# Latent attention: three roots, one weight split and the last two heads' third transpose chunk moved

## The chip, the cores and the metric

The kernel runs on one core of a Trainium2 chip. The metric is the time of one execution of the whole program on the device, in microseconds (us). The matrix engine (TensorE) is PE, its weight loads are PEld, VectorE is DVE, ScalarE is ACT, GpSimd is POOL, and SP is SyncE, whose queue issues the weight loads.

## The reference, cut to what matters

Two blocks of a network run on one sequence of 512 rows of width 1024 in fp32. The first has a gated MLP beside dilated attention, then a feed-forward part. The second has latent attention, a feed-forward part, an mLSTM mixer and a last feed-forward part. The change touches the latent attention alone:

```
cq  = rms_norm(h @ w_dq);            q = (cq @ w_uq)   -> 16 heads of 96
ckv = rms_norm((h @ w_dkv)[:256]);   kv = (ckv @ w_ukv) -> 16 heads: 64 of k, 64 of v
k = [k, shared rotary 32];  q = rms_norm(q)*gain;  k = rms_norm(k)*gain;  rotate the last 32
p = softmax(q k^T * 96**-0.5, key chunk (of 64) <= query chunk)
y = (p v, heads side by side) @ w_o
```

## The kernel before, in words

The program is written by hand for each engine, with semaphores between them; nothing plans the order but the code. Every large product is three fp32r matmuls (high by high, high by low, low by high), so each unit of weights is split once it has landed: `split_hi` (line 399, work at L408, on ACT) writes the rounded part, `split_lo` (line 410, work at L414, on DVE) the rest. A unit is loaded into a slot once the unit before the last in that slot has been split low; SP waits for this in `load_unit` (line 393).

`mla` (lines 2116 to 2552) is the latent attention. The 16 heads (MH) come in four groups of four. Each group g needs four q products and four kv products ("q", g, t and "kv", g, t, one for each tile t of 128 rows), a square of all q and all k (`squares`, L2326 on ACT, POOL's L2404 for k of groups 2 and 3), row sums (`sums`, L2415 on DVE), means (L2419), the square roots (`roots`, L2330 on ACT, Sqrt), their reciprocals and the scaling of k (`norm`, L2423 to L2429 on DVE) and the rotation (`rotate`, L2435 to L2438). Groups 0 and 1 are made ahead of the first head; groups 2 and 3 in among the heads. Before the change `roots(g)` for g = 1, 2, 3 is called at the end of the iterations n = 0, 4 and 8 of ACT's loop over the heads.

One head n takes these steps:
- PE, `scores(n)` (L2240): query tiles in the order 3, 2, 0, 1 against the keys up to the tile's end, so 512, 384, 128 and 256 columns. Tile 3 goes to PSUM bank 0, tiles 2 and 0 to bank 1, tile 1 to bank 2.
- DVE, `mask` (L2447) adds the mask, takes the row maximum and puts the scores in SBUF (SB); `shift` (L2454) makes the bias of the exponential. `masks(n)` is the masks of tiles 2, 0 and 1 and one shift.
- ACT, `exps(n)` (L2337): four exponentials, in place.
- PE, `turn(n, c)` (L2250): the probabilities are transposed in three chunks, of 4, 4 and 2 blocks. Chunks 0 and 2 go to PSUM bank 3, chunk 1 to bank 4. Chunks 0 and 2 are copied to SBUF by ACT (L2384, counted by `pte`, two for each head), chunk 1 by DVE (L2515, counted by `a1`). As chunk 2 goes into the bank of chunk 0, `turn(n, 2)` waits for the copy of chunk 0.
- PE, `values(n)` (L2262): probabilities by values, to bank 6, with a column of ones for the denominators. Tile 3 needs the copy of chunk 0, tile 2 that of chunk 1, tile 1 that of chunk 2.
- DVE, `normed(n)` (L2464, L2466): divides by the denominators.
- Every second head, PE transposes a pair of heads (job "out", L2223), ACT empties it to `norm_T_hi` (L2312) and DVE makes `norm_T_lo` (L2472).

PE's loop runs one head ahead with the scores:

```
scores(n + 1); turn(n, 0); tr q of head n + 2; turn(n, 1); tr k of head n + 2
turn(n, 2); out; values(n); products of a later group
```

"tr" are transposes of q and k (L2218), emptied by ACT (L2316). The jobs ("q", "kv", "tr", "out") take their banks in turn: the first twenty from 5, 7, 4, 6, the others from 5 and 7 (`bank`, L2182). ACT's loop is, for head n: a split at n = 2, 3, 5, 10 and 13 (`SPLITS`, L2184), copy of chunk 0, tr q, copy of chunk 2, tr k, out, `exps(n + 1)`, products, roots or squares. DVE's is: mask of tile 3 of n + 1 and its shift, copy of chunk 1, the other masks of n + 1, out, sums and split, `normed(n)`, the rest of a group's work.

The first heads: after the kv products of group 1 ACT empties the transposes of heads 0 and 1 (`heads01`, L2367), squares k of group 1 (L2369) and then does `exps(0)`. ACT's `split_hi(u0 + 4)` stands between the first and the second kv product of group 1 (L2365), DVE's `split_lo(u0 + 4)` ahead of the masks of head 0 (L2503). The unit u0 + 4 holds the q weights of group 2, first used at n = 1.

The last heads: for n = 15 the turns, the values and the last "out" are handed on (`tail`, L2293) and run between pieces of the product with w_o, whose first piece needs the masks of all heads to be done (`freed`, L2546).

Of the kernel before, what the change touches and what calls it, by code (L numbers as in the profile page):

```python
# [15 lines left out]
P = 128  # L16
# [26 lines left out]
ACT = mybir.ActivationFunctionType  # L43
# [179 lines left out]
def build(nc, A, out, stop_after=99):  # L223
    with ExitStack() as ctx:
# [1891 lines left out]
        def mla(block, CKV, banks):  # L2116
# [63 lines left out]
            def bank(m):  # L2180

                return (5, 7, 4, 6)[m % 4] if m < 20 else (5, 7)[m % 2]  # L2182

            SPLITS = {2: 5, 3: 6, 5: 7, 10: 8, 13: 9}  # L2184

            @block.sync
# [4 lines left out]
            @block.tensor  # L2191
            def _(pe, ev=ev.copy(), tl=tl.copy(), pex=pex.copy(), a1=a1.copy(), pte=pte.copy(), ond=ond.copy(), fs=fs.copy(), ropes=ropes.copy()):
                def job(what):
                    m = idx[what]
                    same = [i for i in range(m) if bank(i) == bank(m)]
                    if same:
                        last = same[-1]
                        pe.wait_ge(ev.sem, ev.at(emptied[last]))
                        if order[last][0] == "out":
                            pe.wait_ge(tl.sem, tl.at(order[last][1] + 1))  # L2200
                    kind = what[0]
                    if kind == "q":
                        ua = u0 + 2 * what[1]
                        if what == ("q", 0, 0):
                            pe.wait_ge(tl.sem, cq_made)
                        pe.wait_ge(w_lo, ua + 1)
                        group_N(pe, ua, 0, 384, 384, 3, PS[:, bank(m), 0:384], what[2], AH, AL)
                    elif kind == "kv":
                        ub = u0 + 2 * what[1] + 1
                        if what == ("kv", 0, 0):  # L2210
                            pe.wait_ge(tl.sem, ckv_made)
                        pe.wait_ge(w_lo, ub + 1)
                        group_N(pe, ub, 0, 512, 512, 2, PS[:, bank(m), :], what[2], AH, AL, k0=3)
                    elif kind == "tr":
                        j, h = what[1:]
                        pe.wait_ge((ropes, fs)[j].sem, (ropes.at(4 * (h // 4) + 2), fs.at(h // 4 + 1))[j])
                        for t in range(NT):
                            mm = pe.transpose(PS[0:MQK, bank(m), t * P:t * P + P], QK[:, h // 4 % 2, j, t, h % 4, :], IDENT[:, :])  # L2218
                        mm.then_inc(tp.sem, 1)
                    else:  # L2220
                        pe.wait_ge(ond.sem, ond.at(2 * what[1] + 2))
                        for t in range(NT):
                            mm = pe.transpose(PS[:, bank(m), t * P:t * P + P], ON[:, t, :], IDENT[:, :])  # L2223
                        mm.then_inc(tp.sem, 1)

                def compressed():
                    pe.wait_ge(xn.sem, ckv_ready)
                    for k in range(2):
                        for t in range(NT):
                            mm = pe.transpose(PS[:, banks[k], t * P:t * P + P], CKV[:, t, k * P:k * P + P], IDENT[:, :])  # L2230
                        mm.then_inc(tp.sem, 1)

                def scores(n):
                    pe.wait_ge(ev.sem, ev.at(emptied[idx[("tr", 1, n)]]))
                    for i, t in enumerate(ORDER):
                        b, c = S_AT[t]
                        w = (t + 1) * P
                        if n and c == 0:
                            pe.wait_ge(smk.sem, smk.at(4 * n - 4 + (1, 3, 4)[b]))
                        pe.matmul(PS[:, b, c:c + w], QT[:, n % 2, t * P:t * P + P], KT[:, n % 2, 0:w],  # L2240
                                  start=True, stop=True).then_inc(sc.sem, 1)

                def turn(n, c):
                    pe.wait_ge(pex.sem, pex.at(4 * n + RAISED[c]))
                    if c == 2:
                        pe.wait_ge(pte.sem, pte.at(2 * n + 1))
                    elif n:
                        pe.wait_ge((pte, a1)[c].sem, (pte.at(2 * n), a1.at(n))[c])
                    for i, (t, j) in enumerate(CHUNKS[c]):
                        mm = pe.transpose(PS[:, 4 if c == 1 else 3, i * P:i * P + P], SB[:, off[t] + j * P:off[t] + j * P + P], IDENT[:, :])  # L2250
                    mm.then_inc(ptr.sem, 1)

                def values(n):
                    if n:
                        pe.wait_ge(ond.sem, ond.at(n))
                    for t in ORDER:
                        if t == 2:
                            pe.wait_ge(a1.sem, a1.at(n + 1))
                        elif t != 0:
                            pe.wait_ge(pte.sem, pte.at(2 * n + (1 if t == 3 else 2)))  # L2260
                        for j in range(t + 1):
                            mm = pe.matmul(PS[:, 6, t * MV1:t * MV1 + MV1], PT[:, off[t] + j * P:off[t] + j * P + P],  # L2262
                                           VN[:, n // 4 % 2, j, n % 4, :], start=j == 0, stop=j == t)
                    mm.then_inc(pvd.sem, 1)

                for m, what in enumerate(fills[0] + fills[1] + heads01):
                    if m == 2:
                        compressed()
                    job(what)
                scores(0)  # L2270
                for n in range(MH):
                    behind, between, before, gemms = jobs_at(n)
                    if n + 1 == MH:
                        break
                    scores(n + 1)
                    turn(n, 0)
                    for what in behind:
                        job(what)
                    turn(n, 1)
                    for what in between:  # L2280
                        job(what)
                    turn(n, 2)
                    for what in before:
                        job(what)
                    values(n)
                    for what in gemms:
                        job(what)

                def last_turn():
                    for c in range(3):  # L2290
                        turn(MH - 1, c)

                tail.extend((last_turn, lambda: values(MH - 1), lambda: job(("out", MH // 2 - 1))))  # L2293

            @block.scalar
            def _(act):
# [64 lines left out]
                squares(1, 0)  # L2361
                for t in range(NT):
                    empty(("kv", 1, t))
                    if t == 0:
                        split_hi(act, u0 + 4)  # L2365
                act.wait_ge(gcol, 16 * 5)
                for what in heads01:  # L2367
                    empty(what)
                squares(1, 1)  # L2369
                exps(0)  # L2370
                for n in range(MH):
# [4 lines left out]
                    for c in (0, 2):  # L2376
                        if c:
                            for what in behind:
                                empty(what)
                        act.wait_ge(ptr.sem, ptr.at(3 * n + c + 1))  # L2380
                        if n:
                            act.wait_ge(pvd.sem, pvd.at(n))
                        w = len(CHUNKS[c]) * P
                        act.activation(PT[:, 4 * c * P:4 * c * P + w], PS[:, 3, 0:w], ACT.Copy).then_inc(pte.sem, 1)  # L2384
                    for what in between + before:
                        empty(what)
                    if n + 1 < MH:
                        exps(n + 1)
                    for what in gemms:
                        empty(what)  # L2390
                    if n % 4 == 0 and g < 4:
                        roots(g)
                    if n % 4 == 2 and g + 1 < 4:
                        squares(g + 1, 0)
                empty(("out", MH // 2 - 1))
# [11 lines left out]
            def _(dve):  # L2407
# [92 lines left out]
                norm(0)  # L2500
                sums(1, 0)
                rotate(1, 0)
                split_lo(dve, u0 + 4)  # L2503
                mask(0, 3)
                shift(0, slice(3, 4))
                masks(0)
                for n in range(MH):
                    g = n // 4 + 1
                    if n + 1 < MH:
                        mask(n + 1, 3)  # L2510
                        shift(n + 1, slice(3, 4))
                    dve.wait_ge(ptr.sem, ptr.at(3 * n + 2))
                    if n:
                        dve.wait_ge(pvd.sem, pvd.at(n))
                    dve.tensor_copy(PT[:, 4 * P:8 * P], PS[:, 4, :]).then_inc(a1.sem, 1)  # L2515
                    if n + 1 < MH:
                        masks(n + 1)
                    if n % 2 == 0 and n:
# [532 lines left out]
```

## Time and profile before

| what | us |
|---|---|
| median of three runs (lowest, highest) | 1930.77 (1930.56, 1930.82) |
| the profiled execution's own time | 1930.67 |
| its span in the trace | 1928.9 |
| PE busy | 1912.6 |
| DVE busy | 1216.5 |
| ACT busy | 944.2 |
| granted TensorE clock over the span | 1.0 |

The span is the time from the first to the last instruction of the profiled execution; the 1.8 us between it and the execution's own time lie around it. A start time in the rows below is in us from the span's start. PE's matmuls are pipelined and their ends are modelled, so a matmul that was waited for shows as a later start. The heads run from about 866 us (scores of head 0) to 1012 us (last pair), and the products of the groups before them from about 841 us.

### The profile page before, as it was taken

The page shows a single profiled execution, that of the slowest core. Times are in us where ns is not written, and L with a number is a line of the kernel's source. Part 1 is how long each engine was busy: PE and PEld are TensorE (multiplying, and loading weights), DVE is VectorE, ACT ScalarE, POOL GpSimd, SP SyncE. Part 2 cuts the span into 40 slices and gives each one's busy share as a digit, 9 for nine tenths or more (in the row PEclk, how much of TensorE's full clock was granted, in tenths as well). Part 3 has the DMA queues.
Part 4 walks back from the last instruction along what each step waited for, and adds up shares of the span by engine and source line. Part 5 has one row for each costly group of instructions (what it writes and reads, how often), then busy time and mean ns, then how long its engine had stood idle before and what let it go on. Part 6 is the DMA issues. An engine that isn't in the chain of part 4 may idle for free.

```text
span 1928.9 us, 23399 instructions
## 1 busy us (share of the span) xinstructions
PE 1912.6 (99%) x9546; PEld 1624.9 (84%) x9546; DVE 1216.5 (63%) x1653; ACT 944.2 (49%) x1335; POOL 50.3 (3%) x85
## 2 busy tenths in 40 slices
PE   8999999999999999999999999999999999999999
PEld 6889998888888888898888888888888889888887
DVE  5645553345767676976745868667634357776867
ACT  5333334234645445568744644435564546453543
POOL 1000000000000000010000000000000000000000
PEclk9999999999999999999999999999999999999999
DMA  7233322322341431311014142241232223414141
GB/s 249 76 98 97 92 68 97 110 99 88 110 139 38 151 114 62 103 59 46 23 44 131 44 153 93 83 153 44 89 110 68 86 66 109 140 58 153 35 140 68
DMA packets 163397, 182.47 MB, mean 95 GB/s; under 512 B 7681, under 2 KB 125014, under 8 KB 163162
## 3 DMA queue, kind: packets, MB, share of 16 engines
q1 hardware_dynamic: 160746, 176.67, 28.4%
q0 software_dynamic: 2528, 4.29, 0.8%
q8 instruction: 76, 1.25, 0.3%
q14 instruction: 31, 0.25, 0.0%
q10 hardware_dynamic: 16, 0.00, 0.0%
HBM read 175.62 MB, written 2.11 MB: 92 GB/s over the span
## 4 chain that ended last, share of the span: by engine, by line
PE 96%; DVE 2%; ACT 1%; issue 0%; DMA 0%; ACTq 0%; DVEq 0%
PE psum L96 29%; PE psum L98 29%; PE psum L97 29%; PE psum L2262 2%; PE psum L2240 2%; PE psum L2693 1%; PE psum L2250 1%; PE psum L566 1%; DVE weights_lo L414 1%; PE psum L2218 1%; PE psum L2681 0%; PE psum L1013 0%; PE psum L984 0%; PE psum L1005 0%; PE psum L994 0%; PE psum L982 0%
## 5 line engine op out<-in xcount | busy, mean ns | idle before, releaser
L96 PE MATMUL psum<-norm_T_hi,weights_hi 128*128 128x512 f32 (+1 forms) x1440 | 538.3, 374 | 0.2 <-DVE weights_lo L414 0.2
L98 PE MATMUL psum<-norm_T_hi,weights_lo 128*128 128x512 f32 (+1 forms) x1440 | 533.6, 371 | 0.0
L97 PE MATMUL psum<-norm_T_lo,weights_hi 128*128 128x512 f32 (+1 forms) x1440 | 533.3, 370 | 0.0
L414 DVE TENSOR_TENSOR weights_lo<-raw_weights,weights_hi 128x2048 fp32r<-128x2048 f32 (+3 forms) x136 | 299.2, 2200 | 234.0 <-ACT weights_hi L408 233.9
L408 ACT ACTIVATE weights_hi<-raw_weights 128x2048 fp32r<-128x2048 f32 (+3 forms) x136 | 249.4, 1834 | 189.4 <-PE psum L98 189.4
L98 PEld LDWEIGHTS psum<-norm_T_hi,weights_lo 128*128 128x128 f32 x1440 | 271.2, 188 | 46.6
L96 PEld LDWEIGHTS psum<-norm_T_hi,weights_hi 128*128 128x128 f32 x1440 | 271.4, 188 | 45.7 <-DVE weights_lo L414 0.5
L97 PEld LDWEIGHTS psum<-norm_T_lo,weights_hi 128*128 128x128 f32 x1440 | 271.4, 188 | 45.5
L96 PE MATMUL psum<-weights_hi,act_T_hi 128*128 128x512 f32 (+1 forms) x528 | 203.9, 386 | 0.0
L98 PE MATMUL psum<-weights_hi,act_T_lo 128*128 128x512 f32 (+1 forms) x528 | 202.9, 384 | 0.0
L97 PE MATMUL psum<-weights_lo,act_T_hi 128*128 128x512 f32 (+1 forms) x528 | 202.9, 384 | 0.0
L414 DVE TENSOR_TENSOR weights_lo<-scratch,weights_hi 128x2048 fp32r<-128x2048 f32 x66 | 151.2, 2291 | 51.4 <-ACT weights_hi L408 51.4
L408 ACT ACTIVATE weights_hi<-scratch 128x2048 fp32r<-128x2048 f32 x66 | 126.1, 1910 | 100.6 <-PE psum L98 100.6
L1698 ACT ACTIVATE scratch<-psum 128x512 f32<-128x512 f32 x96 | 57.2, 596 | 217.8 <-PE psum L98 217.8
L96 PE MATMUL psum<-weights_hi,norm_T_hi 128*128 128x512 f32 (+3 forms) x352 | 127.9, 363 | 0.9 <-DVE norm_T_lo L608 0.5
L97 PE MATMUL psum<-weights_lo,norm_T_hi 128*128 128x512 f32 (+3 forms) x352 | 125.6, 357 | 0.0
L98 PE MATMUL psum<-weights_hi,norm_T_lo 128*128 128x512 f32 (+3 forms) x352 | 125.6, 357 | 0.0
L96 PEld LDWEIGHTS psum<-weights_hi,act_T_hi 128*128 128x128 f32 x528 | 99.2, 188 | 18.8 <-issue 0.3
L98 PEld LDWEIGHTS psum<-weights_hi,act_T_lo 128*128 128x128 f32 x528 | 99.1, 188 | 18.7
L97 PEld LDWEIGHTS psum<-weights_lo,act_T_hi 128*128 128x128 f32 x528 | 99.2, 188 | 18.6
L96 PE MATMUL psum<-weights_hi,feed_operands 128*128 128x512 f32 x288 | 112.2, 390 | 0.0
L97 PE MATMUL psum<-weights_lo,feed_operands 128*128 128x512 f32 x288 | 112.1, 389 | 0.0
(315 smaller groups left out, 2463.9 us busy)
## 6 DMA issues: line engine op xcount, KB each, us to landing
raw_weights<-in_ffn_w_dram SPq DMA_DIRECT2D x32, 1024.0 KB, 5.4
scratch<-in_ffn_w_dram SPq DMA_DIRECT2D x32, 1024.0 KB, 5.4
raw_weights<-in_w_in_dram SPq DMA_DIRECT2D x26, 512.0 KB, 5.1
raw_weights<-in_w_in_dram SPq DMA_DIRECT2D x11, 1024.0 KB, 5.2
raw_weights<-in_w_up_dram SPq DMA_DIRECT2D x8, 1024.0 KB, 6.7
scratch<-in_w_up_dram SPq DMA_DIRECT2D x8, 1024.0 KB, 6.7
raw_weights<-in_w_down_dram SPq DMA_DIRECT2D x8, 1024.0 KB, 5.4
scratch<-in_w_down_dram SPq DMA_DIRECT2D x8, 1024.0 KB, 5.2
```

What stands on the lines that cost most here:

```text
L96: pe.matmul(out, ah, bh, start=start, stop=False, skip_group_check=more)
L97: pe.matmul(out, ah, bl, start=False, stop=False, skip_group_check=more)
L98: return pe.matmul(out, al, bh, start=False, stop=stop, skip_group_check=more)
L408: act.activation(WH[:, u % 2, 0:c], raw(units[u].slot)[:, 0:c], ACT.Copy).then_inc(w_hi, 1)
L414: dve.tensor_tensor(WL[:, u % 2, 0:c], raw(units[u].slot)[:, 0:c], WH[:, u % 2, 0:c].bitcast(F32), SUB).then_inc(w_lo, 1)
L566: mm = pe.transpose(PS[:, bank, q * P:q * P + P], (X if behind else XN)[:, t, k * P:k * P + P], IDENT[:, :])
L1698: act.activation(h, PS[:, up_banks[f % 4], :], ACT.Relu).then_inc(fr.sem, 1)
L2218: mm = pe.transpose(PS[0:MQK, bank(m), t * P:t * P + P], QK[:, h // 4 % 2, j, t, h % 4, :], IDENT[:, :])
L2240: pe.matmul(PS[:, b, c:c + w], QT[:, n % 2, t * P:t * P + P], KT[:, n % 2, 0:w], start=True, stop=True).then_inc(sc.sem, 1)
L2250: mm = pe.transpose(PS[:, 4 if c == 1 else 3, i * P:i * P + P], SB[:, off[t] + j * P:off[t] + j * P + P], IDENT[:, :])
L2262: mm = pe.matmul(PS[:, 6, t * MV1:t * MV1 + MV1], PT[:, off[t] + j * P:off[t] + j * P + P], VN[:, n // 4 % 2, j, n % 4, :], start=j == 0, ...
L2693: mm = pe.matmul(PS[:, 4 + t, 0:LV + 1], place(h, j)[1][:, (t - j) * P:(t - j) * P + P], VN[:, h % 2, j, :], start=j == 0, stop=j == t)
```

## The change

There are three moves; nothing is computed that was not computed before, and each engine has the same instructions.

1. ACT calls `roots(g)` at n = 1, 5 and 9, between the emptied k transposes and `exps(n + 1)`, where it called them at n = 0, 4 and 8 behind everything else.
2. ACT's `split_hi(u0 + 4)` goes from behind the first kv product of group 1 to behind `heads01`, ahead of `squares(1, 1)` and `exps(0)`. DVE's `split_lo(u0 + 4)` goes from before to behind the masks of head 0.
3. For heads 14 and 15 the third chunk is transposed into the bank that the last "out" job takes (bank 7), where it was bank 3. `turn(14, 2)` waits for the job before in that bank (tr k of head 15) instead of for the copy of chunk 0; `turn(15, 0)` and `turn(15, 2)` wait for the copies of head 14 that emptied their banks; the last "out" waits for the copy of the third chunk of head 15. On DVE, in iteration 14, the mask of tile 3 of head 15 and its shift go behind the copy of chunk 1 of head 14.

```
+            def third_bank(n):
+                return 3 if n < MH - 2 else bank(len(order) - 1)
...
                         pe.wait_ge(ond.sem, ond.at(2 * what[1] + 2))
+                        if m == len(order) - 1:
+                            pe.wait_ge(pte.sem, pte.at(2 * MH))
...
                     pe.wait_ge(pex.sem, pex.at(4 * n + RAISED[c]))
-                    if c == 2:
-                        pe.wait_ge(pte.sem, pte.at(2 * n + 1))
+                    if c == 2 and n == MH - 2:
+                        pe.wait_ge(ev.sem, ev.at(emptied[[m for m in range(len(order) - 1) if bank(m) == third_bank(n)][-1]]))
+                    elif c == 2:
+                        pe.wait_ge(pte.sem, pte.at(2 * n + 1 if n < MH - 2 else 2 * n))
                     elif n:
-                        pe.wait_ge((pte, a1)[c].sem, (pte.at(2 * n), a1.at(n))[c])
+                        pe.wait_ge((pte, a1)[c].sem, (pte.at(2 * n if n < MH - 1 else 2 * n - 1), a1.at(n))[c])
...
-                        mm = pe.transpose(PS[:, 4 if c == 1 else 3, ...
+                        mm = pe.transpose(PS[:, (3, 4, third_bank(n))[c], ...
...
                 for t in range(NT):
                     empty(("kv", 1, t))
-                    if t == 0:
-                        split_hi(act, u0 + 4)
                 act.wait_ge(gcol, 16 * 5)
                 for what in heads01:
                     empty(what)
+                split_hi(act, u0 + 4)
                 squares(1, 1)
                 exps(0)
...
-                        act.activation(PT[...], PS[:, 3, 0:w], ACT.Copy).then_inc(pte.sem, 1)
+                        act.activation(PT[...], PS[:, third_bank(n) if c else 3, 0:w], ACT.Copy).then_inc(pte.sem, 1)
                     for what in between + before:
                         empty(what)
+                    if n % 4 == 1 and g < 4:
+                        roots(g)
                     if n + 1 < MH:
                         exps(n + 1)
                     for what in gemms:
                         empty(what)
-                    if n % 4 == 0 and g < 4:
-                        roots(g)
...
                 rotate(1, 0)
-                split_lo(dve, u0 + 4)
                 mask(0, 3)
                 shift(0, slice(3, 4))
                 masks(0)
+                split_lo(dve, u0 + 4)
                 for n in range(MH):
                     g = n // 4 + 1
-                    if n + 1 < MH:
+                    if n + 2 < MH:
                         mask(n + 1, 3)
                         shift(n + 1, slice(3, 4))
...
                     dve.tensor_copy(PT[:, 4 * P:8 * P], PS[:, 4, :]).then_inc(a1.sem, 1)
+                    if n + 2 == MH:
+                        mask(n + 1, 3)
+                        shift(n + 1, slice(3, 4))
```

## Rows read from the trace of the kernel before

**Rows 1.** The page, part 1: busy time, share of the span, instructions.

```profile
PE 1912.6 (99%) x9546; PEld 1624.9 (84%) x9546; DVE 1216.5 (63%) x1653; ACT 944.2 (49%) x1335; POOL 50.3 (3%) x85
```

**Rows 2.** Waits of PE in 820 to 1030: total us, times, longest.

```profile
PE psum L2250 <- ACT scratch L2384: 1.1, 4, 0.3
PE psum L2262 <- DVE scratch L2515: 0.4, 1, 0.4
```

**Rows 3.** Timeline of ACT ahead of head 0: start, us, instruction [idle before, releaser].

```profile
862.27 1.17 ACT L408 ACTIVATE weights_hi<-raw_weights 128x1152 fp32r<-128x1152 f32 x1
863.33 0.38 ACT L2308 ACTIVATE scratch<-psum 128x256 f32<-128x256 f32 x1
...
864.72 0.38 ACT L2308 ACTIVATE scratch<-psum 128x256 f32<-128x256 f32 x1 [0.19 <-PE psum L98]
...
867.55 1.50 ACT L2326 ACTIVATE scratch<-scratch 128x1536 f32<-128x1536 f32 x1
869.07 1.28 ACT L2337 ACT_TABLE_LOAD   x1
870.36 2.29 ACT L2337 ACTIVATE scratch<-scratch,small 128x512 f32<-128x512 f32 x4
```

**Rows 4.** Chain that ended last, 861 to 885: start, us, what.

```profile
866.58 4.61 PE psum L2240 x16
...
871.23 0.66 PE psum L2250 x4
...
875.86 2.21 PE psum L2240 x8
```

**Rows 5.** Timeline of ACT, heads 1 and 2.

```profile
881.05 1.28 ACT L2337 ACT_TABLE_LOAD   x1
...
885.48 0.49 ACT L2303 ACTIVATE scratch<-psum 128x384 f32<-128x384 f32 x1 [0.47 <-PE psum L98]
...
888.08 0.60 ACT L2384 ACTIVATE scratch<-psum 128x512 f32<-128x512 f32 x1 [1.17 <-PE psum L2250]
```

**Rows 6.** Timeline of ACT, heads 5 and 6.

```profile
915.09 1.28 ACT L2330 ACT_TABLE_LOAD   x1
916.38 0.23 ACT L2330 ACTIVATE small<-small 128x32 f32<-128x32 f32 x1
916.52 1.05 ACT L408 ACTIVATE weights_hi<-raw_weights 128x1024 fp32r<-128x1024 f32 x1
917.47 0.58 ACT L2384 ACTIVATE scratch<-psum 128x512 f32<-128x512 f32 x1
...
926.88 0.60 ACT L2384 ACTIVATE scratch<-psum 128x512 f32<-128x512 f32 x1 [2.11 <-PE psum L2250]
```

**Rows 7.** Chain that ended last, head 5.

```profile
918.76 0.70 DVE scratch L2515
...
919.51 1.55 PE psum L2262 x12
```

**Rows 8.** Timeline of ACT, heads 9 and 10.

```profile
957.97 1.28 ACT L2337 ACT_TABLE_LOAD   x1
...
961.46 1.90 ACT L408 ACTIVATE weights_hi<-raw_weights 128x2048 fp32r<-128x2048 f32 x1
963.27 0.57 ACT L2384 ACTIVATE scratch<-psum 128x512 f32<-128x512 f32 x1
```

**Rows 9.** Timeline of PE's weight loads, head 10, third chunk.

```profile
963.95 0.20 PEld L2250 LDWEIGHTS psum<-ident,scratch 128*128 128x128 f32 x2 [0.45 <-issue]
```

**Rows 10.** The same for the third chunks of heads 14 and 15.

```profile
990.22 0.20 PEld L2250 LDWEIGHTS psum<-ident,scratch 128*128 128x128 f32 x2 [0.55 <-issue]
...
999.97 0.20 PEld L2250 LDWEIGHTS psum<-ident,scratch 128*128 128x128 f32 x2 [0.55 <-issue]
```

**Rows 11.** Timelines: DVE's last shift, and PE's first load for w_o.

```profile
992.54 0.16 DVE L2454 SCALAR_TENSOR_TENSOR small<-small 128x3 f32<-128x3 f32 x1
...
993.06 0.19 PEld L96 LDWEIGHTS psum<-weights_hi,norm_T_hi 128*128 128x128 f32 x1
```

More of the change, by code:

```diff
@@ L2182, in bank, with third_bank @@
                 return (5, 7, 4, 6)[m % 4] if m < 20 else (5, 7)[m % 2]
+            def third_bank(n):
+                return 3 if n < MH - 2 else bank(len(order) - 1)
             SPLITS = {2: 5, 3: 6, 5: 7, 10: 8, 13: 9}
@@ L2221, in job @@
                         pe.wait_ge(ond.sem, ond.at(2 * what[1] + 2))
+                        if m == len(order) - 1:
+                            pe.wait_ge(pte.sem, pte.at(2 * MH))
                         for t in range(NT):
@@ L2244, in turn @@
                     pe.wait_ge(pex.sem, pex.at(4 * n + RAISED[c]))
-                    if c == 2:
-                        pe.wait_ge(pte.sem, pte.at(2 * n + 1))
+                    if c == 2 and n == MH - 2:
+                        pe.wait_ge(ev.sem, ev.at(emptied[[m for m in range(len(order) - 1) if bank(m) == third_bank(n)][-1]]))
+                    elif c == 2:
+                        pe.wait_ge(pte.sem, pte.at(2 * n + 1 if n < MH - 2 else 2 * n))
                     elif n:
-                        pe.wait_ge((pte, a1)[c].sem, (pte.at(2 * n), a1.at(n))[c])
+                        pe.wait_ge((pte, a1)[c].sem, (pte.at(2 * n if n < MH - 1 else 2 * n - 1), a1.at(n))[c])
                     for i, (t, j) in enumerate(CHUNKS[c]):
-                        mm = pe.transpose(PS[:, 4 if c == 1 else 3, i * P:i * P + P], SB[:, off[t] + j * P:off[t] + j * P + P], IDENT[:, :])
+                        mm = pe.transpose(PS[:, (3, 4, third_bank(n))[c], i * P:i * P + P], SB[:, off[t] + j * P:off[t] + j * P + P], IDENT[:, :])
                     mm.then_inc(ptr.sem, 1)
@@ L2363, in _ @@
                     empty(("kv", 1, t))
-                    if t == 0:
-                        split_hi(act, u0 + 4)
                 act.wait_ge(gcol, 16 * 5)
@@ L2368, in _ @@
                     empty(what)
+                split_hi(act, u0 + 4)
                 squares(1, 1)
@@ L2383, in _ @@
                         w = len(CHUNKS[c]) * P
-                        act.activation(PT[:, 4 * c * P:4 * c * P + w], PS[:, 3, 0:w], ACT.Copy).then_inc(pte.sem, 1)
+                        act.activation(PT[:, 4 * c * P:4 * c * P + w], PS[:, third_bank(n) if c else 3, 0:w], ACT.Copy).then_inc(pte.sem, 1)
                     for what in between + before:
                         empty(what)
+                    if n % 4 == 1 and g < 4:
+                        roots(g)
                     if n + 1 < MH:
@@ L2390, in _ @@
                         empty(what)
-                    if n % 4 == 0 and g < 4:
-                        roots(g)
                     if n % 4 == 2 and g + 1 < 4:
@@ L2502, in _ @@
                 rotate(1, 0)
-                split_lo(dve, u0 + 4)
                 mask(0, 3)
@@ L2506, in _ @@
                 masks(0)
+                split_lo(dve, u0 + 4)
                 for n in range(MH):
                     g = n // 4 + 1
-                    if n + 1 < MH:
+                    if n + 2 < MH:
                         mask(n + 1, 3)
@@ L2515, in _ @@
                     dve.tensor_copy(PT[:, 4 * P:8 * P], PS[:, 4, :]).then_inc(a1.sem, 1)
+                    if n + 2 == MH:
+                        mask(n + 1, 3)
+                        shift(n + 1, slice(3, 4))
                     if n + 1 < MH:
```

## The prediction

> **What bounds the kernel now.** I read the busy shares first. PE is busy for 1912.6 us of a span of 1928.9 [rows 1]; all its idle time together is 16 us, so a change that removes no matmul can give back only PE's stalls, and only those in its own stage. Then the waits of PE in that stage: four of 0.3 us at L2250 on ACT's copies and one of 0.4 us at L2262 on DVE's copy [rows 2]. That is the whole purse, some 1.5 us by the matmuls' starts, a little more by the weight loads, which stop sooner. The reader should see that the question is less what can be won than what is newly put on the way. For that I read ACT's timeline head by head, with PE's beside it: an ACT row with an idle time in brackets before it had room, a row without one was started by the row above it.
>
> **Part 2, the split before head 0.** Before, `split_hi(u0 + 4)` stands at 862.27 and takes 1.06 us of ACT (862.27 to 863.33). It costs nothing there: at 864.72 ACT idles 0.19 us for PE's last kv product, so it had caught up [rows 3]. The emptied transposes of heads 0 and 1 come behind that product whatever stood before, so moving the split away from it starts nothing sooner; scores(0) stay at 866.58 [rows 4]. At its new place there is no such room. From the last of those transposes to exps(0) ACT runs without idling: squares at 867.55, table load at 869.07, exps at 870.36 [rows 3]. A split put in at 867.55 moves all three by 1.06, exps(0) to 871.4.
> Who waits for exps(0)? turn(0, 0), at 871.23, which is 0.87 behind 870.36. It would start at 872.3. PE was ready for it at about 871.2: the two heads' scores take 4.61 us from 866.58, where twice the 2.21 of one head is 4.42 [rows 4]. The missing 0.19 is the wait for head 0's masks, which DVE's moved `split_lo` now shortens; but PE then only waits sooner for exps(0). So the gain of DVE's move is 0 and the cost of ACT's is 1.06 less the at most 0.04 that the chain left between scores and turn: **+1.05 us**. Everything behind in head 0 (the copy of chunk 0 follows exps(0) on ACT) moves with it. DVE's `split_lo` comes in time: it then lies where DVE waited for turn(0, 0), its unit is used only at n = 1, and the load that SP holds behind it (two units on) is used at n = 3. Bounds: from -0.19 (ACT's split is hidden after all and the masks' wait goes) to +1.06.
>
> **Part 1, the roots.** A roots call costs ACT a table load and the Sqrt: from 915.09 to 916.52, 1.43 us [rows 6], and the next exps another load of 1.28, in both kernels. The number of loads is the same; what moves is the 1.43, from ahead of the copies of heads 1, 5 and 9 to ahead of exps of heads 2, 6 and 10.
> What is gained: at n = 5 the copy of chunk 0 started at 917.47, straight after the split and the roots [rows 6], and the third chunk was late. But behind it values(5) waited for DVE's copy of chunk 1, which ran from 918.76, and went on at 919.51 [rows 7]. DVE's order there is unchanged and did not wait for ACT's roots, so that end stands: 0 gained; at most the 0.4 of [rows 2]. At n = 1 and 9 the copy came at PE's pace; 0.
> What it costs: at n = 2 exps(2) come 1.43 later; behind them ACT had idled 0.47 and, before the copy of chunk 0, 1.17 [rows 5]: 1.64 of room against 1.43, so 0, with 0.2 to spare. At n = 6 the idle time before the copy alone is 2.11 [rows 6]: 0. At n = 10 there is none. No product stands between; exps(10) are followed by a split of 2048 columns at 961.46 and this by the copy of chunk 0 at 963.27, all without idling [rows 8], and PE already waited 0.45 for it before the third chunk [rows 9]. The 1.43 goes through in full: copy at 964.7, third chunk at 965.4, then the pair and values(10). **+1.43 us.** DVE's norm waits for the roots: at n = 1, 5 and 9 they still end before it starts, so 0. Bounds: -0.4 (gain at head 5, nothing lost at 10) to +1.5.
> The Trainium skill ("ScalarE: Activation LUTs", What ACT_TABLE_LOAD costs) says that a switch takes the load of 1283 ns and a drain of 1380 ns more. This trace does not agree: the load at 915.09 is followed by the Sqrt at 916.38, and the one at 869.07 by the exponential at 870.36, 1.29 us each [rows 3, 6]. By the skill's figure the move would cost 2.8 us at n = 10, by the rows 1.43.
>
> **Part 3, the last two heads.** The third chunk's weights were loaded 0.55 us late in head 14 and again in head 15 [rows 10]: chunk 1 follows chunk 0 at once (no q and k transposes are left to put between), so PE is back at bank 3 before ACT has copied chunk 0. With a bank of its own the wait goes. The new waits are on things long done: tr k of head 15 was emptied in head 13; the copies of head 14 lie ahead of a whole piece of the w_o product, and so does the copy of head 15 that the last "out" now waits for. Head 15: **-0.53**. Head 14: PE would reach w_o's first load at 993.06 - 0.54 = 992.52, and that load waits for the last mask, just ahead of the shift at 992.54 [rows 11]. DVE's moved mask and shift change their order, not their sum, so this end stays and eats about 0.1 of it: **-0.45**. exps(15) hang on the same shift and have a whole piece of product before they are used. Bounds: 0 (the wait is another) to -1.1.
>
> **The sum.** +1.05 + 1.43 - 0.53 - 0.45 = +1.5 us. Against the profiled execution's own time, 1930.67 (span 1928.9 and 1.8 around it; 0.10 under the median of 1930.77), that is 1932.2. Behind this stage PE is the bound again and nothing absorbs or adds: the SP loads hang on splits that move with PE.
>
> **The rivals.**
> (a) ACT has more room than its rows say at one of the two places, say because PE is held by something else at head 10: one of the two costs goes. 1930.7 with the split's cost alone, 1931.1 with the roots'. For it: each rests on one chain; against: both chains show no idle time.
> (b) Both are hidden, and the change does what its moves suggest: masks' wait 0.19 and head 5's 0.4 gained on top of the last heads' 0.98. 1929.1; without the two small ones 1929.7. Against: [rows 7] and the unbroken ACT rows.
> (c) The last two heads gain nothing (the third chunk waits for its exponentials or its start costs the same in another bank), with the rest as forecast: 1933.2.
> (d) Slower: ACT's room at n = 2 and n = 6 is not there. The place is ACT's stretch from the k transposes of heads 1 and 5 to the next copy of chunk 0; the price 1.43 each; it decides once the idle time there, 1.64 and 2.11, is below the 1.43 (the product of n = 1 must be emptied behind the later exps, so 0.47 of it is the doubtful part). +1.05 + 3 x 1.43 - 0.98 = +4.4, 1935.0.
> (e) A load is followed by as much idle time again, where the loads stand back to back (Sqrt's, then Exp's), as they never do in this trace: one load more, +1.28 at n = 10, 1933.5. This is the case in which the skill's drain would be real. Every load of the stage speaks against it.
>
> **How the numbers follow.** A measurement of this kernel tells about 0.2% (3.9 us) from no change; nearly every case lies within it. Forecast 0.60, own range 1931.6 to 1932.7 (0.2 for the masks' end, 0.3 for n = 2 overflowing); (a) 0.14; (b) 0.12; (c) 0.06; (d) 0.03; (e) 0.02; something unseen 0.03. The range reaches over (a), nearly all of (b) and (c): 1929.1 to 1933.3. Faster by over 0.2% 0.01, slower by over 0.2% 0.04, within 0.95.
>
> **What would show it.** In the profile after: exps of head 0 start about 4.8 us behind the start of scores(0), where it was 3.8, with PE idle before its first L2250 for over a microsecond; at head 10 the third chunk's load shows about 1.9 us of idle where 0.45 stood; the idle of 0.55 before the third chunks of heads 14 and 15 is gone; ACT's idle before the copy of chunk 0 in head 2 has shrunk to a few tenths; values(5) still wait for L2515. The prediction is wrong if exps(0) keep their distance from scores(0), if head 10's third chunk is no later than before, or if PE waits in heads 2 or 6 where it did not.

## The result and the profile after

| | median us | lowest to highest | executions |
|---|---|---|---|
| before | 1930.76 | 1930.37 to 1931.59 | 22 |
| changed | 1934.23 | 1932.23 to 1937.94 | 22 |

The ratio of changed to before is 1.0019, 95% interval 1.0013 to 1.0025: slower by 3.5 us. The forecast was 1932.2, its range ended at 1933.3. The kernel before spreads over 1.2 us; the changed one has two clusters. Eleven executions lie at 1932.23 to 1933.11 (median 1932.52), nine at 1935.35 to 1936.34, two at 1937.59 and 1937.94, and nothing between them. Every execution of the lower cluster shows a mean granted clock of 1.0, every one above it 0.997 or 0.998. The profiled execution, 1935.65 with a span of 1933.8, is one of the upper ones.

The first rows are ACT's timeline of the changed kernel ahead of head 0, to be laid beside [rows 3] (L408 is the split, L2334 the squares, L2345 the exponentials).

```profile
867.63 1.18 ACT L408 ACTIVATE weights_hi<-raw_weights 128x1152 fp32r<-128x1152 f32 x1
868.68 1.50 ACT L2334 ACTIVATE scratch<-scratch 128x1536 f32<-128x1536 f32 x1
870.20 1.28 ACT L2345 ACT_TABLE_LOAD   x1
871.49 2.29 ACT L2345 ACTIVATE scratch<-scratch,small 128x512 f32<-128x512 f32 x4
```

The split takes 1.05 us between the transposes' copies and the squares, with no idle time anywhere in the stretch, and exps(0) start 4.83 us behind the scores of head 0, where it was 3.78. In head 2 the room just held: the copy of chunk 0 still waited for PE, by 0.20 us where it was 1.17 [rows 5]. In head 9 and 10 it did not (compare [rows 8]):

```profile
959.11 1.28 ACT L2338 ACT_TABLE_LOAD   x1
960.40 0.23 ACT L2338 ACTIVATE small<-small 128x32 f32<-128x32 f32 x1
960.65 1.28 ACT L2345 ACT_TABLE_LOAD   x1
961.95 2.29 ACT L2345 ACTIVATE scratch<-scratch,small 128x512 f32<-128x512 f32 x4
964.14 1.89 ACT L408 ACTIVATE weights_hi<-raw_weights 128x2048 fp32r<-128x2048 f32 x1
965.94 0.57 ACT L2391 ACTIVATE scratch<-psum 128x512 f32<-128x512 f32 x1
```

What PE makes of both, in its weight loads: turn(0, 0) is held for 1.52 us, the third chunk of head 10 for 1.99 where [rows 9] had 0.45, and the third chunks of heads 14 and 15 come in one row of ten with the chunks before them; the 0.55 of [rows 10] is gone.

```profile
872.36 0.42 PEld L2258 LDWEIGHTS psum<-ident,scratch 128*128 128x128 f32 x4 [1.52 <-ACT scratch L2345]
...
966.63 0.20 PEld L2258 LDWEIGHTS psum<-ident,scratch 128*128 128x128 f32 x2 [1.99 <-issue]
...
994.66 1.23 PEld L2258 LDWEIGHTS psum<-ident,scratch 128*128 128x128 f32 x10
...
1003.94 1.24 PEld L2258 LDWEIGHTS psum<-ident,scratch 128*128 128x128 f32 x10
```

So far this is the forecast. What is new stands right behind head 10's wait, in the chain (values of head 10, scores of head 12, then values and scores of the next head):

```profile
967.80 3.48 PE psum L2270 x20
971.28 4.24 PE psum L2246 x8
...
977.49 2.18 PE psum L2270 x20
979.67 2.21 PE psum L2246 x8
```

The same twenty and eight matmuls take 3.48 and 4.24 us once and 2.18 and 2.21 us the next time: 3.33 us more. The stretches of the same profile (busy time of each engine with its count, then PE's granted clock, DMA share, GB/s) say why:

```profile
962.00:966.00 4.00, 2.90 (x22) 2.37 (x20) 3.89 (x10) 4.00 (x6) 0.00 (x0) 1.00 0.02 4
966.00:968.00 2.00, 1.27 (x10) 1.06 (x11) 0.60 (x3) 1.98 (x6) 0.00 (x0) 1.00 0.00 0
968.00:970.00 2.00, 2.00 (x13) 2.00 (x13) 1.42 (x2) 2.00 (x5) 0.00 (x0) 0.61 0.00 0
970.00:975.00 5.00, 5.00 (x14) 3.29 (x14) 1.98 (x3) 0.72 (x2) 0.00 (x0) 0.50 0.45 142
976.00:980.00 4.00, 4.00 (x36) 3.76 (x35) 2.92 (x13) 3.64 (x7) 0.00 (x0) 1.00 0.00 0
```

The granted clock is 0.50 from 970 to 975, its lower level of 1.2 GHz, and 1.0 before and after. It falls some two microseconds after PE has resumed work, following the stretches in which PE was busy for 2.90 of 4 us and 1.27 of 2. The 3.3 us are about the distance between the clusters: 1935.65 less 1932.52 is 3.1, and the nine of the middle group have their median at 1935.88, 3.4 above. The Trainium skill ("TensorE: Matmul & The Clock Gate", Part 1: The HAM clock gate) says that the matrix clock has two levels, full and half, that a hardware monitor of recent activity picks, and that the moment of a change varies from execution to execution; the trace agrees on the levels (1.00 and 0.50 above); the two clusters go further, since here not only the moment but whether the clock falls at all varies.

### The profile page after: what moved, and what is told of

It reads as the page before. It is cut to its first block, busy times and chain, and to the rows that moved or that the text cites. A ratio compares the mean times of both kernels' runs of the same rounds, so it can differ in the third digit from the quotient of the medians.

```text
span 1933.8 us, 23399 instructions
## 1 busy us (share of the span) xinstructions
PE 1915.4 (99%) x9546; PEld 1627.5 (84%) x9546; DVE 1216.2 (63%) x1653; ACT 943.9 (49%) x1335; POOL 50.4 (3%) x85
## 4 chain that ended last, share of the span: by engine, by line
PE 95%; DVE 2%; ACT 2%; issue 0%; DMA 0%; ACTq 0%; DVEq 0%
PE psum L96 29%; PE psum L98 29%; PE psum L97 29%; PE psum L2270 2%; PE psum L2246 2%; PE psum L2703 1%; PE psum L2258 1%; PE psum L566 1%; DVE weights_lo L414 1%; PE psum L2222 1%; PE psum L2691 0%; PE psum L1013 0%; PE psum L1005 0%; PE psum L984 0%; PE psum L994 0%; PE psum L982 0%
## 5 line engine op out<-in xcount | busy, mean ns | idle before, releaser
L408 ACT ACTIVATE weights_hi<-raw_weights 128x2048 fp32r<-128x2048 f32 (+3 forms) x136 | 249.5, 1834 | 189.4 <-PE psum L98 189.4
L408 ACT ACTIVATE weights_hi<-scratch 128x2048 fp32r<-128x2048 f32 x66 | 126.1, 1910 | 100.6 <-PE psum L98 100.6
L96 PE MATMUL psum<-weights_hi,feed_operands 128*128 128x512 f32 x288 | 112.2, 390 | 0.0
L98 PE MATMUL psum<-weights_hi,feed_operands 128*128 128x512 f32 x288 | 112.1, 389 | 0.0
```

The lines of the kernel that those rows point to most:

```text
L96: pe.matmul(out, ah, bh, start=start, stop=False, skip_group_check=more)
L98: return pe.matmul(out, al, bh, start=False, stop=stop, skip_group_check=more)
L408: act.activation(WH[:, u % 2, 0:c], raw(units[u].slot)[:, 0:c], ACT.Copy).then_inc(w_hi, 1)
```

## The experiments

The theory after the result: the two costs are as forecast (together with the gain of the last heads they give the lower cluster), and head 10's longer wait at times lets PE's clock fall, which costs 3 us or more on top of them. Rival A puts the fall on the wait ahead of head 0, rival B on the chip, rival D on something else in head 9 and 10 than PE's idleness. The kernel before ran beside each; its medians were 1930.87, 1930.73 and 1930.69, so two medians compare to about 0.2 us.

**1. The roots back.** `e1_roots_undone`, against the changed kernel:

```
-                    if n % 4 == 1 and g < 4:
-                        roots(g)
                     if n + 1 < MH:
                         exps(n + 1)
                     for what in gemms:
                         empty(what)
+                    if n % 4 == 0 and g < 4:
+                        roots(g)
```

> The roots are back at heads 0, 4 and 8; the other two moves stay. Theory (PE's idle time at head 10, 1.99 us in the changed kernel's trace, lets the TensorE clock fall to its lower level in about half of the executions): no execution shows a granted clock under 1.0, and the time is the changed kernel's lower cluster, about 1932.6, less the 1.54 us that head 10's wait grew by: 1931.1 in all executions. Rival A (the idle time ahead of head 0, 1.52 us, is what lets the clock fall): about half of the executions still lie 3 us above the rest. Rival B (the fall is a state of the chip on that day): executions of the kernel before show it too.

Measured: 1930.91 (1930.57 to 1931.46, eleven executions, none above). PE's wait ahead of head 0 is untouched:

```profile
872.17 0.42 PEld L2258 LDWEIGHTS psum<-ident,scratch 128*128 128x128 f32 x4 [1.52 <-ACT scratch L2345]
```

So 1.52 us of waiting there never let the clock fall in eleven executions: rival A is out as a cause by itself.

**2. The split back.** `e2_split_undone`: both halves of part 2 as before, roots and banks changed.

```
                     empty(("kv", 1, t))
+                    if t == 0:
+                        split_hi(act, u0 + 4)
...
-                split_hi(act, u0 + 4)
                 squares(1, 1)
...
+                split_lo(dve, u0 + 4)
                 mask(0, 3)
                 shift(0, slice(3, 4))
                 masks(0)
-                split_lo(dve, u0 + 4)
```

> ACT's split and DVE's split of the first heads are back where they were; roots and banks stay as changed. Theory: the lower cluster at 1932.6 - 1.1 = 1931.5, and about half of the executions some 3 us above it with a granted clock of 0.998, since head 10's idle time is untouched. Rival A: all at 1931.5 with the clock at 1.0.

Measured: seven executions at 1931.12 to 1931.91, one at 1934.56, three at 1936.13 to 1936.30. The lower seven (median 1931.20) are 0.3 under the expectation; four lie above, one of them by 3.4 us and three by 5, with mean clocks of 0.998 and 0.997. Head 10's wait is 1.99 us here too, while the one ahead of head 0 is back at 0.46, so head 10's is enough for the upper executions. All 33 executions of the kernel before on the same chip lay at 1930.45 to 1931.42: rival B is out.

**3. The banks alone.** `e3_banks_alone`: both edits above together, so that only part 3 is left.

> Only the last two heads' part of the change. Theory: 1930.8 - 1.0 = 1929.8, clock 1.0 in all; the idle time of 0.55 us ahead of the third chunks of heads 14 and 15 is gone. Rival (the last part gives nothing because another wait takes its place): 1930.8.

Measured: 1929.65 (1929.33 to 1929.96). The gain is 1.2 us. In its profile the distance from head 14's first chunk (988.95) to w_o's first load is 3.94 us, where it was 4.40 (988.66 to [rows 11]'s 993.06): 0.46 gained. The load starts 0.04 us into the last shift, so right behind the last mask, which is what it waits for:

```profile
992.85 0.16 DVE L2462 SCALAR_TENSOR_TENSOR small<-small 128x3 f32<-128x3 f32 x1
...
992.89 0.19 PEld L96 LDWEIGHTS psum<-weights_hi,norm_T_hi 128*128 128x128 f32 x1
```

**4. Room for head 10.** `e4_split_at_11`: the changed kernel with `SPLITS = {2: 5, 3: 6, 5: 7, 11: 8, 13: 9}`.

> The changed kernel with the split of head 10's turn made in head 11 (ACT and DVE), so that roots and their loads at head 9 stay but head 10's copy no longer stands behind a split of 1.8 us. Theory: head 10's third chunk waits at most 0.2 us, the time is 1932.6 - 1.9 = 1930.7 and the clock stays at 1.0. Rival A (head 0's idle time): 1930.7 in half of the executions, 3 us more in the others. Rival C (the back-to-back table loads themselves cost more than their rows): above 1932.

Measured: 1930.52 (1930.29 to 1931.68), none above. The moved roots stay, their two loads stand back to back, and head 10's third chunk waits 0.18:

```profile
965.33 0.20 PEld L2258 LDWEIGHTS psum<-ident,scratch 128*128 128x128 f32 x2 [0.18 <-issue]
```

Two microseconds lower than the lower cluster, and the upper one gone: the cost sat in the split of 1.8 us standing behind the moved roots, as the forecast had it, not in the loads.

**5. The wait filled.** `e5_wait_filled`: the changed kernel, and PE works while it waits.

```
                 def turn(n, c):
+                    if (n, c) == (10, 2):
+                        pe.wait_ge(ond.sem, ond.at(10))
+                        for _ in range(16):
+                            pe.transpose(PS[:, 6, 384:512], IDENT[:, :], IDENT[:, :])
                     pe.wait_ge(pex.sem, pex.at(4 * n + RAISED[c]))
```

> The changed kernel, with 16 transposes of the identity into unused columns of bank 6 between head 10's k transposes and its third chunk: PE works through 1.75 us of the 1.99 us that it waited there, ACT's and DVE's order is untouched. Theory (PE's idleness at head 10 lets the clock fall): all executions at the lower cluster of the changed kernel, 1932.4 to 1933, clock 1.0. Rival D (something else of that stretch, ACT's two loads or the order of the copies, goes with the slower executions): about half of them stay 3 us higher.

Measured: 1932.23 (1932.04 to 1932.60), all eleven. PE's loads there (L2253 is the filling):

```profile
964.48 1.78 PEld L2253 LDWEIGHTS psum<-ident 128*128 128x128 f32 x16
966.48 0.20 PEld L2262 LDWEIGHTS psum<-ident,scratch 128*128 128x128 f32 x2 [0.23 <-issue]
```

and its stretch behind, which the changed kernel ran at 0.50:

```profile
970.00:975.00 5.00, 5.00 (x37) 4.24 (x36) 4.17 (x12) 2.69 (x7) 0.00 (x0) 1.00 0.51 151
```

More work for PE, the third chunk no later than before, and the upper cluster is gone. It is PE's idleness, not ACT's order: this is the run that tells the two apart. Runs 6 and 11, on the same chip, did show the fall, so the chip is no reason for its absence here.

**6. The wait made by other means.** `e6_late_copy`: banks alone, and on ACT, in head 10, behind the split:

```
+                    for _ in range(1 if n == 10 else 0):
+                        act.activation(SQ, SQ, ACT.Square)
```

> The last two heads' part alone, with one Square of 1536 columns on ACT (1.4 us, its result unused) ahead of head 10's copy of the first chunk; no roots and no split moved. Theory: head 10's third chunk waits 0.45 + 1.4 = 1.85 us, the lower cluster is 1929.7 + 1.4 = 1931.1, and a good part of the executions, from a third to two thirds, lies 3 to 5 us above it with a clock under 1.0. Rival D (the idle time alone is not enough): all at 1931.1.

Measured: six executions at 1930.88 to 1931.45, five at 1934.29 to 1934.99. No roots, loads or first-head split are moved, PE waits 1.82 us, and both clusters are back, 3.1 us apart by their medians:

```profile
965.15 0.20 PEld L2258 LDWEIGHTS psum<-ident,scratch 128*128 128x128 f32 x2 [1.82 <-issue]
```

**7. Half of it.** `e7_half_late`: the same with `act.activation(SQ[:, 0:768], SQ[:, 768:1536], ACT.Square)`.

> As the run with the late copy, with a Square of 768 columns, about 0.75 us: head 10's third chunk waits 1.2 us. Both theories give 1929.7 + 0.75 = 1930.4 for the lower cluster. If the share of slower executions grows with the idle time, some of them lie higher, fewer than with the whole Square; if the fall needs the longer wait, none.

Measured: 1930.28 (1930.20 to 1930.97), none above, at a wait of 1.18 us. At head 10 the wait of 1.82 us gave five of eleven, that of 1.18 none; ahead of head 0 one of 1.52 gave none of eleven. Sizes between were not tried, nor was a wait of 1.8 us or more made at another place, so neither the shortest wait that does it nor a part of head 10's surroundings in it is settled.

**8. A better kernel.** `e8_best`: part 3; the split at 11; roots of group 2 at head 5, the others as before the change; DVE's `split_lo(u0 + 4)` behind head 0's masks, ACT's split at its old place; and DVE's copy of chunk 1 ahead of the next mask in two more heads:

```
-                    if n + 2 < MH:
+                    if n + 2 < MH and n not in (5, 9):
                         mask(n + 1, 3)
                         shift(n + 1, slice(3, 4))
...
-                    if n + 2 == MH:
+                    if n + 2 == MH or n in (5, 9):
```

> The last two heads' part, the split of head 10 made in head 11, the roots of group 2 at head 5 (the others where they were before), and DVE's copy of chunk 1 ahead of the next head's mask in heads 5 and 9 as well. Theory by the stalls of the trace: 1929.7 less 0.45 (head 10), 0.58 (values of head 9) and 0.4 to 0.6 (head 5): 1928.1, clock 1.0. Rival (the next head's masks come later and the wait moves to its exponentials or scores): 1929.0 to 1929.7.

Measured: 1927.58 (1927.39 to 1928.11), 0.5 under the expectation; ratio to before 0.9984, interval 0.9975 to 0.9992. In head 5 nothing waits between the chunks and the values (L2258 the third chunk, L2270 all twenty loads of the values):

```profile
917.62 0.25 PEld L2258 LDWEIGHTS psum<-ident,scratch 128*128 128x128 f32 x2
917.84 2.31 PEld L2270 LDWEIGHTS psum<-scratch 128*128 128x128 f32 x20
```

**9 and 10. Its parts.** `e9_banks_split11`: part 3 and the split at 11 only. `e10_dve_first`: `e8_best` with all roots where they were before the change.

> The last two heads' part, and the split of head 10 made in head 11; roots, first heads and DVE's order as before the change. Theory: 1929.65 less the wait of head 10 that stays without the moved roots (0.45 ahead of the third chunk; the 0.3 ahead of the pair stays only if it follows from it): 1929.0 to 1929.2. Rival (the split only makes another copy late, in head 11): 1929.6.

> As the run before, with DVE's copy of chunk 1 ahead of the next head's mask in heads 5 and 9, and DVE's split of the first heads behind its masks; the roots all as before the change. Against the best kernel this lacks only the roots of group 2 moved to head 5. Theory: the wait of values in head 9 (0.58) goes, that in head 5 (0.2) too, the third chunk of head 5 stays 0.41 late: 1929.1 - 0.8 = 1928.3, 0.4 above... 0.7 above the best kernel's 1927.6. Rival (the roots' move at head 5 gives nothing even once DVE is early): 1927.6.

Measured: 1929.23 (1928.87 to 1929.76) and 1928.48 (1927.90 to 1928.93). So by the medians, from 1929.65, the split at 11 gives 0.4, DVE's order (its two copies and its first split) 0.75, and the roots at head 5, once DVE is early, 0.9. The runs stood on three chips and medians compare to 0.2 us, so the traces are the better measure of single parts. Two weight loads that wait for DVE in every trace, near 810 and near 1380 us, enclose the stage. They are 570.80 us apart in run 3, 570.17 in run 9, 569.28 in run 10 and 568.85 in run 8: 0.63 for the split, 0.89 for DVE's order, 0.43 for the roots at head 5, where the third chunk had waited 0.41. In the given change the same move gave nothing at head 5, as its values then waited 0.58 for DVE where it was 0.20.

**11. The upper executions' trace.** `e11_split_undone_again`: run 2's kernel, one execution.

> The kernel of the second run once more, for its trace: some of its executions lay 3 us above the lower cluster and some 5 us. If the profiled execution is one of them, theory says that the granted clock falls to its lower level behind head 10's wait and stays there for about 6.8 us (3 us more) or about 10 us (5 us more). If it is one of the lower cluster, it shows 1.0 throughout and settles nothing.

Measured: 1934.48, a mean clock of 0.998. The fall is the changed kernel's over again, behind a wait of 1.98 us:

```profile
967.00:969.00 2.00, 2.00 (x12) 2.00 (x11) 1.62 (x2) 2.00 (x5) 0.00 (x0) 0.51 0.00 0
969.00:974.00 5.00, 5.00 (x14) 3.33 (x14) 1.88 (x3) 0.52 (x2) 0.00 (x0) 0.51 0.48 151
975.00:979.00 4.00, 4.00 (x34) 3.74 (x33) 3.02 (x13) 3.64 (x8) 0.00 (x0) 1.00 0.00 0
```

That shows the 3 us case in a second kernel. No execution of the 5 us case was caught in a trace, so what makes it longer is open.

## Why the prediction was wrong, by its own steps

**Part 2, +1.05: right.** With the roots back, scores(0) to turn(0, 0) takes 5.70 us (866.47 to 872.17), before 4.65 [rows 4]: 1.05. By the medians of runs 1 and 3 the part costs 1.26, by the distance between the two enclosing loads (runs 9 and 10) 1.12, 571.92 against 570.80; the 0.2 more of the medians is no larger than medians compare to. The cover that the split had was real, its new place had none, and DVE's earlier masks gained PE nothing.

**Part 1, +1.43: right in place, a little small.** Head 10's wait grew by 1.54. The lower cluster of run 2 against run 3 gives 1.55, the two enclosing loads 1.64, and run 4 shows that the split behind the roots was the exposed piece. No gain at head 5 (the copy of chunk 0 became early, waiting 0.71 for PE, and the values waited for DVE instead), none lost at heads 2 and 6: right, with 0.20 us of idle time left before head 2's copy, the forecast's "0.2 to spare". Table loads cost 1.28 and no drain: rival (e) fell.

**Part 3, -0.98: right.** 0.46 in head 14 by the trace (forecast 0.45), a row of ten without a gap in head 15; 1.05 by the two enclosing loads (571.85 before, 570.80 in run 3), 1.2 by the medians.

**The sum, +1.5.** It is the lower cluster: 1932.52 against 1932.2. It is in the profiled upper execution too, whose span is 4.9 us longer than before: less the 3.33 at the lower clock that leaves 1.6. **The step that failed** is the sentence behind it, "Behind this stage PE is the bound again and nothing absorbs or adds". A wait was priced at its own length and no more. PE waited for 1.99 us in head 10, and in 11 of 22 executions the clock fell behind it, 3.3 us more each, 5 in two. That is the median's 1.7 us over the lower cluster (1934.23 against 1932.52; half the executions on either side, so the median falls between clusters). That it came out there is luck: with one more execution of 22 in the lower cluster the median would have been 1933.1 or less, inside the range, and the mechanism missed all the same. None of the rivals held a case in which a wait costs more than its length; rival (d), the slowest, put the surplus on further exposed roots at heads 2 and 6, and there were none.

The table of the kernel before had the hint: a clock of 1.0, with a longest PE wait in this stage of 0.58 us. Behind the program's first nine microseconds, which hold waits of 6.1 and 2.0, no load of PE waits longer than 0.97 us (at 1477.88 and 1519.83). Behind those two early waits the matmuls do look slow, although the clock's column reads 1.00 there. Those of 512 columns start 0.43 us apart at first and 0.23 from 13.03 us on:

```profile
12.31 0.63 PE L97 MATMUL psum<-weights_lo,norm_T_hi 128*128 128x512 f32 x1
12.74 0.45 PE L98 MATMUL psum<-weights_hi,norm_T_lo 128*128 128x512 f32 x1
13.03 0.39 PE L96 MATMUL psum<-weights_hi,norm_T_hi 128*128 128x512 f32 x1
13.26 0.39 PE L97 MATMUL psum<-weights_lo,norm_T_hi 128*128 128x512 f32 x1
```

That is nearly the ratio of the two levels, so a mean clock of 1.0 in a table doesn't prove that the clock was full at the start.

A change forecast to make a PE wait of 1.9 us in head 10 left what the trace before could speak for, and a fall of the clock behind it should have been a rival with its own chance and price. The price could be read: the matmuls of the seven microseconds behind the wait at half speed.

## What to carry to other kernels

In a kernel whose matrix engine hardly pauses, list what a change does to its longest single pause as well as to their sum: run 1, with pauses of 1.52 and 0.44 us, kept its clock in all eleven executions, run 2, with one of 1.99, lost it in four of eleven. If such a pause can't be avoided, harmless matmuls into an unused part of a bank can hold the clock; in run 5 they did so at no cost (1932.23 against the lower cluster's 1932.52). And an instruction moved on a busy engine is priced by the idle time between its new place and the next instruction that PE waits for; an order pays only once both engines that feed a product are early (runs 8 and 10).

## What the runs showed that was not expected

- With a single wait of PE of 1.82 to 1.99 us in head 10, 21 of 45 executions show a mean granted clock under 1.0 and the longer time (changed kernel 11 of 22, run 2 4 of 11, run 6 5 of 11, run 11 once in one). Two of the 21 were traced, and both fell right behind that wait; where the others fell is inferred. Waits of 1.52 us ahead of head 0 (run 1) and 1.18 us in head 10 (run 7) were not, in eleven executions each.
- The fall begins after PE has resumed, and lasted some seven microseconds in both traces that show it; PE was busy throughout.
- The same program lands in either cluster from one execution to the next, so a median of a few executions can miss 3 us either way.
